# A hybrid attention and feed-forward step: the last two phases put in one block, with the feed-forward's first tiles in attention memory that is no longer read

## The chip, the cores and the metric

One core of one Trainium2 chip. The metric is the device time of one execution, in microseconds (us), taken as the median of several executions. The profile is one further execution under the hardware profiler.

## What is computed

One layer of a streaming encoder, for a prompt of 2048 rows and for 32 rows of a running stream, all of width 1024 and all in fp32. A matmul operand is split into a high and a low part, and every product is three matmuls (high·high, high·low, low·high).

```
h = rmsnorm(x, norm_mix_pre);  z = h @ w_in         # cut into the two groups' q, k, v, gate
ret_out  = silu(rg) * rms(retention(rq, rk, rv))    # 4 heads, width 512
diff_out = differential_attention(dq, dk, dv)       # 4 heads, width 512, block-causal mask
mix = concat(ret_out, diff_out) @ w_out
x   = x + rmsnorm(mix, norm_mix_post)               # "x1" below
u   = rmsnorm(x, norm_ffn_pre) @ w_up               # 1024 -> 4096
f   = square(relu(u)) @ w_down                      # 4096 -> 1024
y   = x + rmsnorm(f, norm_ffn_post)
```

## The kernel before

The kernel has four phases: retention, the projections of the attention group with the decode rows' attention, the prompt's attention with the output projection (`mix_phase`), and the feed-forward (`ffn_phase`). Each phase owns its SBUF tensors and semaphores and one block, in which each engine runs its own instruction stream. At the end of a phase (`phase`, L30) the semaphores are cleared and all engines meet at a barrier (L36).

**Attention (`mix_phase`).** Rows go in 16 tiles of 128 and each tile has four heads, so there are 64 items. One item is scores, exponentials, combination, transposes of the weights, and the weighted sum of V (`weigh`, L1493) which counts up `s_o`. The output projection of one tile of mixed rows j is a transpose (`mixT`, L1448), the split into `mTh` on ScalarE (L1221) and `mTl` on VectorE (`mT_lo`, L1354), and four quarters of 12 matmuls (`quarter`, L1465): quarters 0 and 1 fill the left 512 columns in bank `Y`, quarters 2 and 3 the right. j = 0 is the 32 decode rows, j = 16 is the last 128 prompt rows; below these last rows are "row tile 16". After each half ScalarE copies `Y` out (`y_out`, L1235), then sums squares (`meansq_y`, L1240); GpSimd takes the root (`rstd_y`, L1157); VectorE scales (`y_norm`, L1363) and adds the residual (`residual`, L1370), which gives x1. SyncE stores x1 to a scratch in HBM (`finish`, L1119) and waits for that store, and then loads the next residual rows (`residual_rows`, L1115) once ScalarE has read the buffer (`meansq_x`, L1248). GpSimd's `rstd_x` (L1163) leaves the root of each x1 row for the feed-forward. These tensors are live to the end: the w_out splits, the mixed rows, `mTh`, `mTl`, `xr`, `y`, the gain. Dead once the last `weigh` has run are `KT`, `V`, `S`, `AT`, `kn`, `qn`, `qT`, 114 KB per partition by their shapes.

**The tail of attention,** after the last item, is written by hand in program order on each engine. TensorE: quarters 2 and 3 of row tile 15, `mixT` of row tile 16, its four quarters. ScalarE: `y_out` and `meansq_y` of 15, `mTh` of 16, `meansq_x` of 15, then `y_out` (twice), `meansq_y`, `meansq_x` of 16. VectorE: `y_norm` and `residual` of 15, `mT_lo` of 16, `y_norm` and `residual` of 16.

**The feed-forward (`ffn_phase`).** The 17 row tiles are in two blocks, tiles 0 to 7 and tiles 8 to 16. For each block all the weights are read once, in 16 groups of 256 hidden columns. SyncE loads x1 tiles into four slots (`x_tile`, L1666), the gain (L1672) and half-pieces of weights into `raw`. Per row tile: VectorE normalises (`norm_x`, L1886), TensorE transposes (`x_transpose`, L2056, two banks of four), ScalarE writes `hTh` (`x_hi`, L1762), VectorE writes `hTl` (`x_lo`, L1892). The two transpose banks are single: `x_transpose(t)` waits for `x_lo(t-1)`. Weights are split by ScalarE (`up_hi`, L1751) and VectorE (`up_lo`, L1873). The first group's up products (`first_up`, L2065, four units of 24 matmuls for block 0) are woven with the transposes of tiles 4 to 7; behind each unit run `relu` (ScalarE, L1782), `square` (VectorE, L1913), `hid_hi` (ScalarE, L1787) and `hid_lo` (VectorE, L1919). After that TensorE alternates a group's up and down products (L2065, L2101), and VectorE adds the down products into `facc` (L1940).

The order at the start of block 0, which the change touches, is on VectorE:

```
norm_x(0) norm_x(1) x_lo(0) norm_x(2) x_lo(1) norm_x(3) up_lo(0) x_lo(2) norm_x(4) x_lo(3) norm_x(5)
x_lo(4) norm_x(6) square(0) x_lo(5) norm_x(7) hid_lo(0) x_lo(6) square(1) x_lo(7) hid_lo(1) ...
```

On ScalarE it is x_hi(0), x_hi(1), up_hi, x_hi(2) to x_hi(4), relu(0), x_hi(5), hid_hi(0), x_hi(6), relu(1), x_hi(7), hid_hi(1). On TensorE it is transposes 0 to 3, half of first_up(0), transpose 4, the other half, transpose 5, half of first_up(1), transpose 6, the other half, transpose 7, first_up(2), first_up(3).

Of the kernel before, what the change touches and what calls it, by code (L numbers as in the profile page):

```python
# [8 lines left out]
F32 = mybir.dt.float32  # L9
# [34 lines left out]
class Kept:  # L44


    def __init__(self, nc, tiles):
        self.ident = nc.alloc_sbuf_tensor("kept_ident", [P, P], F32)
        self.rstd_x = nc.alloc_sbuf_tensor("kept_rstd_x", [P, tiles], F32)
# [888 lines left out]
def mix_phase(nc, banks, keep, seq, dec, x_p, x_s, q_scratch, ret_scratch, mixd_scratch, k_p, v_p, w_out, gain,  # L938
# [8 lines left out]
    with phase(nc) as ctx:  # L947
        def sb(name, shape, dt=F32):
            return ctx.enter_context(nc.sbuf_tensor(f"mix_{name}", shape, dt))

        def sem(name):
            return nc.alloc_semaphore(f"mix_{name}")

        SP_, T, O, Y = banks[0:4], banks[4:6], banks[6], banks[7]
        wt = Weights(nc, ctx, "mixw", 2, 8, staged=False)
        KT = sb("KT", [P, 4, seq])
        V = sb("V", [P, nt, N])
        Sall = sb("S", [P, 4 * seq])
        S = [[Sall[:, (2 * b + m) * seq:(2 * b + m + 1) * seq] for m in range(2)] for b in range(2)]

        assert nt >= 10
        wt.raw = [V[:, nt - 8 + 4 * i:nt - 4 + 4 * i, :] for i in range(2)]
        AT = sb("AT", [P, nt, P])
        kn = [sb(f"kn{u}", [P, N]) for u in range(2)]
        qn = sb("qn", [P, N])
        qTs = [sb(f"qT{u}", [P, 4, P]) for u in range(2)]
        mix = sb("mix", [P, 1024])
        mTh, mTl = sb("mTh", [P, 8, P], F32R), sb("mTl", [P, 8, P], F32R)
        xr, y, gain_b = sb("xr", [P, 1024]), sb("y", [P, 1024]), sb("gain", [P, 1024])
        oscs, junk = [sb(f"osc{b}", [P, HD]) for b in range(2)], sb("junk", [P, 1024], BF16)  # L970
        half = sb("half", [P, 1])
        mx = [sb(f"mx{b}", [P, 2, 5]) for b in range(2)]
        nm = [sb(f"nm{b}", [P, 2]) for b in range(2)]
        l = [sb(f"l{b}", [P, 2]) for b in range(2)]
        rl = [sb(f"rl{b}", [P, 2]) for b in range(2)]
        r = [sb(f"r{b}", [P, 1]) for b in range(2)]
        stats = sb("head_stats", [P, 4])
        sos, mos = [stats[:, b:b + 1] for b in range(2)], [stats[:, 2 + b:3 + b] for b in range(2)]
        ro = [sb(f"rstd_o{b}", [P, 1]) for b in range(2)]
        sy, my, ry = sb("sy", [P, 1]), sb("my", [P, 1]), sb("ry", [P, 1])  # L980
        sx, mean_x = sb("sx", [P, 1]), sb("mean_x", [P, 1])

        s_gain, s_half, s_pad = sem("gain_loaded"), sem("half_set"), sem("padding_set")
        s_kq = [sem("kq_loaded0"), sem("kq_loaded1")]
        s_q = sem("q_loaded")
        s_vl = [sem(f"v_loaded{t}") for t in range(nt)]
        s_ret = sem("ret_loaded")
        s_x = sem("x_loaded")
        s_x1 = sem("x1_ready")
        s_stored = sem("x1_stored")  # L990
        s_ktr = sem("k_and_q_transposed")
        s_tfree = [sem("T0_free"), sem("T1_free")]
        s_qk = sem("pair_bank_filled")
        s_sc = sem("pair_bank_read")
        s_neg = sem("masked_corner_set")
        s_nm = sem("neg_max")
        s_e = sem("exp")
        s_rl, s_r = sem("recip_sums"), sem("ratio")
        s_A = sem("combined")
        s_ATp = sem("AT_psum")  # L1000
        s_o = sem("o_psum")
        s_osc = sem("o_scaled")
        s_so, s_mo, s_ro = sem("o_sumsq"), sem("o_meansq"), sem("o_rstd")
        s_mix = sem("mix_head")
        s_mTh = sem("mixT_hi")
        s_yp, s_y = sem("y_psum"), sem("y_sbuf")
        s_sy, s_my, s_ry, s_yn = sem("y_sumsq"), sem("y_meansq"), sem("y_rstd"), sem("y_normed")
        s_sx, s_mx, s_rx = sem("x1_sumsq"), sem("x1_meansq"), sem("x1_rstd")

        wv = w_out.rearrange("(k p) n -> k p n", p=P)  # L1010
        kv = k_p.rearrange("(n p) h d -> n p (h d)", p=P)
        vv = v_p.rearrange("(n p) h d -> n p (h d)", p=P)
        qv = q_scratch.rearrange("(n p) c -> n p c", p=P)
        rv = ret_scratch.rearrange("(n p) c -> n p c", p=P)
        xv = x_p[0].rearrange("(n p) d -> n p d", p=P)
        x1v = x1_scratch.rearrange("(n p) d -> n p d", p=P)

        def rows(j):
            return P if j else dec

        def width(t):
            return (t + 1) * P

        def chunks(t):
            return [(c, min(N, width(t) - c)) for c in range(0, width(t), N)]

        def groups(t):
            return [range(g, min(g + 4, t + 1)) for g in range(0, t + 1, 4)]

        def early(n):  # L1030
# [1201 lines left out]
```

## Time and profile before

| | us |
|---|---|
| median of 3 executions (lowest, highest) | 3084.81 (3082.12, 3088.74) |
| the profiled execution: its own time | 3086.13 |
| its span, first to last instruction | 3084.4 |
| mean granted TensorE clock | 0.972 |

| engine | busy us | share of the span | instructions |
|---|---|---|---|
| TensorE, matmul | 2897.8 | 94% | 14977 |
| TensorE, weight load | 2386.1 | 77% | 14977 |
| VectorE | 1493.9 | 48% | 3000 |
| ScalarE | 925.3 | 30% | 1838 |
| GpSimd | 286.0 | 9% | 420 |

All times are from the start of the span. In a timeline row the columns are start, duration, engine (PE is TensorE, PEld its weight load, DVE is VectorE, ACT is ScalarE, POOL is GpSimd, SPq is SyncE's DMA queue), the line of the kernel, the instruction, "output <- inputs", the shape, the count of merged instructions, and in brackets the engine's idle time before it with what ended it. A granted clock of 1.00 is 2.4 GHz and 0.50 is 1.2 GHz.

### The profile page before, as it was taken

The page shows a single profiled execution, that of the slowest core. Times are in us where ns is not written, and L with a number is a line of the kernel's source. Part 1 is how long each engine was busy: PE and PEld are TensorE (multiplying, and loading weights), DVE is VectorE, ACT ScalarE, POOL GpSimd, SP SyncE. Part 2 cuts the span into 40 slices and gives each one's busy share as a digit, 9 for nine tenths or more (in the row PEclk, how much of TensorE's full clock was granted, in tenths as well). Part 3 has the DMA queues.
Part 4 walks back from the last instruction along what each step waited for, and adds up shares of the span by engine and source line. Part 5 has one row for each costly group of instructions (what it writes and reads, how often), then busy time and mean ns, then how long its engine had stood idle before and what let it go on. Part 6 is the DMA issues. An engine that isn't in the chain of part 4 may idle for free.

```text
span 3084.4 us, 39331 instructions
## 1 busy us (share of the span) xinstructions
PE 2897.8 (94%) x14977; PEld 2386.1 (77%) x14977; DVE 1493.9 (48%) x3000; ACT 925.3 (30%) x1838; POOL 286.0 (9%) x420
## 2 busy tenths in 40 slices
PE   5999996899978999999699999999989999999997
PEld 4888885677856777766578888888879899898895
DVE  3223332333236877777444454444465444544446
ACT  3222222222125666666322111211132111121112
POOL 0122211111112111110000000000021000000003
PEclk8999998899989999999799999999999999999998
DMA  4111102332432211110321111111133111111112
GB/s 148 35 34 34 34 21 85 129 120 96 145 104 99 80 59 55 56 37 27 115 83 43 54 45 50 41 54 41 41 118 103 55 41 41 41 46 49 41 55 99
DMA packets 105660, 204.63 MB, mean 66 GB/s; under 512 B 11024, under 2 KB 47888, under 8 KB 105552
## 3 DMA queue, kind: packets, MB, share of 16 engines
q1 hardware_dynamic: 103248, 194.79, 19.1%
q0 software_dynamic: 2304, 8.39, 0.8%
q8 instruction: 69, 1.13, 0.1%
q14 instruction: 39, 0.32, 0.0%
HBM read 168.28 MB, written 34.87 MB: 66 GB/s over the span
## 4 chain that ended last, share of the span: by engine, by line
PE 48%; DVE 2%; DMA 0%; ACT 0%; issue 0%; SPq 0%
PE bank L2101 24%; PE bank L2065 23%; DVE ffn_facc L1899 1%; PE bank L2056 0%; DVE ffn_upl L1873 0%; DVE ffn_facc L1940 0%; DVE ffn_hTl L1892 0%; DVE ffn_x L1886 0%; DMA ffn_raw<-in_w_up_dram 0%; DMA ffn_gain_x<-in_norm_ffn_pre_dram 0%; DVE ffn_dnl L1880 0%; DMA ffn_x<-x_scratch 0%; ACT ffn_hTh L1762 0%; ACT ffn_relu L1782 0%; DVE ffn_facc L1906 0%
## 5 line engine op out<-in xcount | busy, mean ns | idle before, releaser
L1940 DVE TENSOR_TENSOR ffn_facc<-bank,ffn_facc 128x512 f32<-128x512 f32 x510 | 346.1, 689 | 243.7 <-PE bank L2101 242.5
L2065 PE MATMUL bank<-ffn_hTh,ffn_uph 128*128 128x352 f32 (+1 forms) x1280 | 451.0, 352 | 8.7 <-DVE ffn_upl L1873 5.5
L2065 PE MATMUL bank<-ffn_hTl,ffn_uph 128*128 128x352 f32 (+1 forms) x1280 | 449.6, 351 | 0.0
L2065 PE MATMUL bank<-ffn_hTh,ffn_upl 128*128 128x352 f32 (+1 forms) x1280 | 449.3, 351 | 0.0
L2101 PE MATMUL bank<-ffn_dnh,ffn_hidh 128*128 128x512 f32 x1088 | 430.3, 396 | 9.4 <-DVE ffn_dnl L1880 6.2
L2101 PE MATMUL bank<-ffn_dnh,ffn_hidl 128*128 128x512 f32 x1088 | 430.9, 396 | 0.0
L2101 PE MATMUL bank<-ffn_dnl,ffn_hidh 128*128 128x512 f32 x1088 | 429.9, 395 | 0.0
L1913 DVE SCALAR_TENSOR_TENSOR ffn_relu<-bank,ffn_relu 128x352 f32<-128x352 f32 (+1 forms) x160 | 94.6, 591 | 484.4 <-ACT ffn_relu L1782 484.2
L2065 PEld LDWEIGHTS bank<-ffn_hTh,ffn_uph 128*128 128x128 f32 x1280 | 241.1, 188 | 33.7 <-issue 7.7
L2065 PEld LDWEIGHTS bank<-ffn_hTl,ffn_uph 128*128 128x128 f32 x1280 | 241.3, 188 | 23.7
L2065 PEld LDWEIGHTS bank<-ffn_hTh,ffn_upl 128*128 128x128 f32 x1280 | 241.0, 188 | 22.6
L2101 PEld LDWEIGHTS bank<-ffn_dnh,ffn_hidh 128*128 128x128 f32 x1088 | 205.8, 189 | 59.3 <-DVE ffn_dnl L1880 6.9
L1757 ACT ACTIVATE ffn_dnh<-ffn_raw 128x1024 fp32r<-128x1024 f32 x64 | 64.5, 1053 | 616.7 <-PE bank L2101 605.5
L1782 ACT ACTIVATE ffn_relu<-bank 128x352 f32<-128x352 f32 (+1 forms) x160 | 82.8, 517 | 535.7 <-PE bank L2065 535.7
L2101 PEld LDWEIGHTS bank<-ffn_dnl,ffn_hidh 128*128 128x128 f32 x1088 | 205.2, 189 | 47.8
L2101 PEld LDWEIGHTS bank<-ffn_dnh,ffn_hidl 128*128 128x128 f32 x1088 | 205.3, 189 | 47.5
L185 PE MATMUL bank<-retw_whi,retp_hTh 128*128 128x512 f32 x544 | 216.8, 399 | 25.7 <-DVE ret_rope_b L395 16.6
L185 PE MATMUL bank<-retw_whi,retp_hTl 128*128 128x512 f32 x544 | 213.8, 393 | 0.0
L185 PE MATMUL bank<-retw_wlo,retp_hTh 128*128 128x512 f32 x544 | 213.7, 393 | 0.0
L1303 DVE TENSOR_SCALAR_CACHE_REDUCE mix_S<-bank 128x512 f32<-128x512 f32 (+4 forms) x320 | 175.0, 582 | 64.6 <-PE bank L1437 31.5
L185 PE MATMUL bank<-dpw_whi,dpp_hTh 128*128 128x512 f32 x408 | 164.4, 403 | 8.9 <-DVE dpw_wlo L175 8.9
L1203 ACT ACTIVATE mix_S<-mix_S,mix_nm 128x128 f32<-128x128 f32 (+15 forms) x128 | 153.7, 1201 | 45.2 <-DVE mix_nm L1317 44.9
(196 smaller groups left out, 4392.3 us busy)
## 6 DMA issues: line engine op xcount, KB each, us to landing
ffn_raw<-in_w_up_dram SPq DMA_DIRECT2D x64, 512.0 KB, 4.4
ffn_raw<-in_w_down_dram SPq DMA_DIRECT2D x64, 512.0 KB, 4.1
ffn_x<-x_scratch SPq DMA_DIRECT2D x24, 512.0 KB, 4.3
retp_x<-in_x_prompt_dram SPq DMA_DIRECT2D x16, 512.0 KB, 3.6
retw_raw<-in_w_in_dram SPq DMA_DIRECT2D x8, 1024.0 KB, 5.1
dpp_x<-in_x_prompt_dram SPq DMA_DIRECT2D x16, 512.0 KB, 4.9
dp_kst<-in_cache_diff_k_dram SPq DMA_DIRECT2D x32, 256.0 KB, 2.9
mix_xr<-in_x_prompt_dram SPq DMA_DIRECT2D x16, 512.0 KB, 3.3
```

The source lines that it names most:

```text
L185: last = self.nc.tensor.matmul(out, l[:, k, :], r[:, c, k, :], start=(k == 0 and q == 0), stop=(k == kt - 1 and q == 2))
L1203: nc.scalar.activation(S[n % 2][m][:, 0:width(t)], S[n % 2][m][:, 0:width(t)], ACT.Exp, bias=nm[n % 2][:, m:m + 1], accum_out=l[n % 2][:, ...
L1303: last = nc.vector.tensor_scalar(dst[:, c:c + whole], src[:, 0:whole], 1.0, None, ALU.mult, ALU.max, accum_out=mx[b][:, m, i + 1:i + 2])
L1757: nc.scalar.activation(dnh[:, i, :], raw[i][:], ACT.Copy).then_inc(s_whi, 1)
L1782: nc.scalar.activation(rh[i % 2][:, 0:w], bank[:, 0:w], ACT.Relu).then_inc(s_r, 1)
L1899: nc.vector.scalar_tensor_tensor(out=facc[:, i, :], in0=facc[:, i, :], scalar=rf[:, t:t + 1], in1=gain_b[:], op0=ALU.mult, op1=ALU.mult).t ...
L1913: nc.vector.scalar_tensor_tensor(out=rh[i % 2][:, 0:w], in0=bank[:, 0:w], scalar=0.0, in1=rh[i % 2][:, 0:w], op0=ALU.max, op1=ALU.mult).th ...
L1940: nc.vector.tensor_tensor(out=part, in0=Dn[i % s.rd][:], in1=part, op=ALU.add).then_inc(s_add, 1)
L2065: last = nc.tensor.matmul(bank[:, 0:w], l[:, k, f * P:(f + 1) * P], r[:, k, c:c + w], start=(k == 0 and q == 0), stop=(k == 7 and q == 2))
L2101: last = nc.tensor.matmul(Dn[i % s.rd][:], l[:, c:c + P], r[:, f, n * N:(n + 1) * N], start=(f == 0 and q == 0), stop=(f == FG - 1 and q = ...
```

## The change

`mix_phase` and `ffn_phase` become two stages of one block. Each engine's stream for attention is a generator that stops at named points of its tail; the feed-forward's stream resumes it at chosen places, so the two orders are woven together per engine. The barrier and the semaphore clearing between the two phases are gone. Everything before the tail keeps its order.

The memory of the feed-forward starts at the address of attention's. `hTh`, `hTl`, the x slots, `gain_x`, `raw`, `uph`, `upl` and the second gain come first (114 KB by their shapes) and lie in the dead tensors; `hid`, `relu`, `dnh`, `dnl` lie in the w_out splits; `facc` lies over the rest. Small tensors are packed, `half` is shared, and `rstd_x` has one column more.

The woven orders, attention's steps in brackets:

- SyncE: wait for the last `weigh`; x tile 0, gain, x tiles 1 to 3, first up pieces; [store x1 of 15, load residual rows of 16]; x tiles 4 to 7; [store x1 of 16]; second gain; second up pieces; x tiles 8 to 11.
- VectorE: norm_x(0); [mT_lo of 16]; norm_x(1); [y_norm and residual of 15]; x_lo(0), and on as before to hid_lo(0); [y_norm and residual of 16]; four memsets that stood at the phase's start; x_lo(6), and on as before.
- ScalarE: [y_out, meansq_y of 15, mTh of 16]; x_hi(0), x_hi(1), up_hi; [meansq_x of 15, y_out left half of 16]; x_hi(2), x_hi(3); [y_out right half, meansq_y of 16]; x_hi(4), relu(0), x_hi(5), hid_hi(0); [meansq_x of 16]; x_hi(6), and on as before.
- TensorE: [quarters of 15, mixT of 16]; transposes 0 and 1; [quarters 0 and 1 of 16]; transposes 2 and 3; [quarters 2 and 3 of 16]; first_up(0), and on as before.
- GpSimd: attention's stream, then the feed-forward's.

```diff
-    with phase(nc) as ctx:                      # in mix_phase and in ffn_phase
+    U, Dn = (banks[0:4] if before_it.last_pair == 0 else banks[2:4] + banks[0:2]), banks[4:8]
 def sync(sp, mixing):
+        sp.wait_ge(s_o, ntot)                   # the last weigh
+        yield "attention ended"
         finish(nt - 1)
         residual_rows(nt)
+        yield "last rows asked for"
         finish(nt)
...
+        next(mixing)
         x_tile(0)
         sp.dma_start(gain_x[:], gain_pre.to_broadcast([P, 1024])).then_inc(s_gain, 16)
         for t in (1, 2, 3):
             x_tile(t)
         for i in range(2):
             piece_up(0, i)
+        next(mixing)
         for t in (4, 5, 6, 7):
             x_tile(t)
+        next(mixing, None)
+        sp.wait_ge(before_it.s_rx, before_it.roots)
+        sp.dma_start(gain_b[:], gain_post.to_broadcast([P, 1024])).then_inc(s_gain_f, 16)
 def vector(dve, mixing):
+        next(mixing)                            # to the last mix_head
+        dve.wait_ge(s_gain, 16)
         norm_x(0)
+        next(mixing)                            # mT_lo(nt)
         norm_x(1)
+        next(mixing)                            # y_norm(nt - 1), residual(nt - 1)
         x_lo(0)
...
         hid_lo(s, 0, 0, 0, fu)
+        next(mixing, None)                      # y_norm(nt), residual(nt)
+        for e in range(2):
+            for part in range(2):
+                nc.vector.memset(hidden_flat[e][part][:, FG * tokens:].bitcast(F32), 0.0).then_inc(s_pad, 1)
         x_lo(6)
...
         down_lo(w0 + 4)
+        if s.b == 0:
+            dve.wait_ge(before_it.s_stored, before_it.stores)
+            dve.wait_ge(before_it.s_rx, before_it.roots)
 def scalar(act, mixing):
+        next(mixing)                            # to mT_hi(nt)
         x_hi(0)
         x_hi(1)
         up_hi(1)
+        next(mixing)                            # meansq_x(nt - 1), y_out(nt, 0)
         x_hi(2)
         x_hi(3)
+        next(mixing)                            # y_out(nt, 1), meansq_y(nt)
         x_hi(4)
         relu(s, 0, 0, fu)
         x_hi(5)
         hid_hi(s, 0, 0, 0, fu)
+        next(mixing, None)                      # meansq_x(nt)
         x_hi(6)
 def tensor(pe, mixing):
+        next(mixing)                            # to mixT(nt)
+        pe.wait_ge(before_it.s_sc, before_it.read_pairs)
+        x_transpose(0)
+        x_transpose(1)
+        next(mixing)                            # quarters 0, 1 of nt
+        x_transpose(2)
+        x_transpose(3)
+        next(mixing, None)                      # quarters 2, 3 of nt
         first_up(s, 0, range(0, 4))
...
+        pe.wait_ge(before_it.s_y, before_it.halves)
+def mix_ffn_phase(nc, banks, keep, mix_args, ffn_args):
+    with phase(nc) as ctx:
+        keep.s_half = nc.alloc_semaphore("half_set")
+        with ExitStack() as first:
+            mix = mix_stage(nc, first, banks, keep, *mix_args)
+        ffn = ffn_stage(nc, ctx, banks, keep, mix, *ffn_args)
+        with nc.Block() as block:
+            @block.sync
+            def _(sp):
+                ffn.sync(sp, mix.sync(sp))
...
```

## Rows read from the trace of the kernel before

**Rows 1.** The page: shares of the chain that ended last, by engine.
```profile
PE 48%; DVE 2%; DMA 0%; ACT 0%; issue 0%; SPq 0%
```

**Rows 2.** Busy time by stretch: stretch, length, each engine's busy us and count, clock, DMA.
```profile
1497.00:1505.00 8.00, 7.64 (x24) 5.87 (x24) 0.11 (x1) 0.39 (x3) 0.55 (x1) 0.73 0.32 118
1505.00:1511.00 6.00, 5.45 (x24) 4.43 (x24) 0.00 (x0) 0.50 (x1) 0.00 (x0) 1.00 0.00 0
1511.00:1527.00 16.00, 0.29 (x2) 0.00 (x0) 3.84 (x7) 3.30 (x7) 1.20 (x3) 0.62 0.41 143
1527.00:1541.00 14.00, 7.79 (x32) 6.18 (x32) 12.88 (x16) 6.45 (x10) 0.00 (x0) 0.50 0.80 294
1600.00:2200.00 600.00, 600.00 (x2589) 485.49 (x2588) 279.77 (x383) 113.97 (x161) 0.00 (x0) 1.00 0.15 47
```

**Rows 3.** TensorE's waits, 1484 to 1577: total us, times, longest.
```profile
PE bank L2056 <- DVE ffn_x L1886: 16.2, 1, 16.2
PE bank L1465 <- DVE mix_mTl L1354: 5.7, 1, 5.7
PE bank L2065 <- DVE ffn_upl L1873: 5.5, 1, 5.5
PE bank L2056 <- DVE ffn_hTl L1892: 4.3, 3, 2.9
```

**Rows 4.** Timeline of the tail of attention.
```profile
1481.71 2.84 PE L1493 MATMUL bank<-mix_V,mix_AT 128*128 128x128 f32 x24
1484.33 0.33 SPq L1115 DMA_DIRECT2D mix_xr<-in_x_prompt_dram  x1
1492.54 1.06 ACT L1221 ACTIVATE mix_mTh<-bank 128x512 fp32r<-128x512 f32 x2
1493.30 1.28 DVE L1363 SCALAR_TENSOR_TENSOR mix_y<-mix_y,mix_ry,mix_gain 128x1024 f32<-128x1024 f32 x1 [6.66 <-POOL mix_ry L1157]
1494.68 1.23 DVE L1370 TENSOR_TENSOR mix_xr<-mix_xr,mix_y 128x1024 f32<-128x1024 f32 x1
1495.83 1.28 DVE L1354 TENSOR_TENSOR mix_mTl<-bank,mix_mTh 128x512 fp32r<-128x512 f32 x2
1516.64 1.06 ACT L1248 ACTIVATE mix_junk<-mix_xr 128x1024 bf16<-128x1024 f32 x1 [3.31 <-DVE mix_xr L1370]
1518.10 0.55 POOL L1163 TENSOR_TENSOR kept_rstd_x<-mix_mean_x,mix_half 128x1 f32<-128x1 f32 x1 [4.14 <-ACT mix_mean_x L1252]
```

**Rows 5.** Timeline of the start of the feed-forward.
```profile
1520.85 0.43 SPq L1672 DMA_DIRECT2D ffn_gain_x<-in_norm_ffn_pre_dram  x1
1526.13 2.54 DVE L1886 SCALAR_TENSOR_TENSOR ffn_x<-ffn_x,kept_rstd_x,ffn_gain_x 128x1024 f32<-128x1024 f32 x2 [5.01 <-DMA ffn_gain_x<-in_norm_ffn_pre_dram]
1527.47 1.97 PE L2056 MATMUL bank<-kept_ident,ffn_x 128*128 128x128 f32 x8 [16.18 <-DVE ffn_x L1886]
1541.04 0.76 PE L2065 MATMUL bank<-ffn_hTh,ffn_uph 128*128 128x512 f32 x1 [1.50 <-DVE ffn_hTl L1892]
1546.02 1.04 PE L2056 MATMUL bank<-kept_ident,ffn_x 128*128 128x128 f32 x8
1546.66 1.09 ACT L1762 ACTIVATE ffn_hTh<-bank 128x512 fp32r<-128x512 f32 x2 [6.48 <-PE bank L2056]
1553.52 0.68 DVE L1919 TENSOR_TENSOR ffn_hidl<-ffn_relu,ffn_hidh 128x512 fp32r<-128x512 f32 x1
1559.78 0.50 PE L2065 MATMUL bank<-ffn_hTh,ffn_uph 128*128 128x512 f32 x1 [1.74 <-DVE ffn_hTl L1892]
```

**Rows 6.** The two issues of `raw` between 1519 and 1535, us to landing.
```profile
DMA to landing us min/median/max: 8.8/9.2/9.7
```

**Rows 7.** Timeline of a restart of TensorE near the end of the kernel.
```profile
3037.01 0.58 PE L2101 MATMUL bank<-ffn_dnh,ffn_hidh 128*128 128x512 f32 x1 [3.54 <-DVE ffn_dnl L1880]
3037.39 0.63 PE L2101 MATMUL bank<-ffn_dnl,ffn_hidh 128*128 128x512 f32 x1
3037.82 0.63 PE L2101 MATMUL bank<-ffn_dnh,ffn_hidl 128*128 128x512 f32 x1
```

More of the change, by code:

```diff
@@ new lines, in mix_stage @@
+    AT = sb("AT", [P, nt, P])
+    kn = [sb(f"kn{u}", [P, N]) for u in range(2)]
+    qn = sb("qn", [P, N])
+    qTs = [sb(f"qT{u}", [P, 4, P]) for u in range(2)]
+    assert nt >= 10
+    wt = Weights(nc, ctx, "mixw", 2, 8, staged=False)
+    wt.raw = [V[:, nt - 8 + 4 * i:nt - 4 + 4 * i, :] for i in range(2)]
+    mix = sb("mix", [P, 1024])
+    mTh, mTl = sb("mTh", [P, 8, P], F32R), sb("mTl", [P, 8, P], F32R)
+    xr, y, gain_b = sb("xr", [P, 1024]), sb("y", [P, 1024]), sb("gain", [P, 1024])
@@ new lines, in mix_stage, with pair_banks, plan_transposes, bank_of @@
+    plan_pairs()
+    def pair_banks(u):
+        return SP_[2 * (u % 2)], SP_[2 * (u % 2) + 1]
+    t_use = {}
+    def plan_transposes():
+        i = itertools.count()
+        t_use["k", 0], t_use["q", 0] = next(i), next(i)
+        for n, (t, h) in enumerate(items):
+            for g in range(len(groups(t))):
+                t_use["A", n, g] = next(i)
+            if h == 0 and t + 1 < nt:
+                t_use["k", t + 1], t_use["q", t + 1] = next(i), next(i)
+    plan_transposes()
+    def bank_of(use):
+        return T[t_use[use] % 2]
@@ new lines, in ffn_stage @@
+    uph, upl = sb("uph", [P, 8, GW], F32R), sb("upl", [P, 8, GW], F32R)
+    gain_b = sb("gain_f", [P, 1024])
+    hidden_flat = [[sb(f"hid{n}{u}", [P, FG * tokens + P - dec], F32R) for n in "hl"] for u in range(2)]
+    rh = [sb(f"relu{i}", [P, N]) for i in range(2)]
+    dnh, dnl = sb("dnh", [P, FG, 1024], F32R), sb("dnl", [P, FG, 1024], F32R)
+    facc = sb("facc", [P, nb_max, 1024])
+    junk = sb("junk", [P, 1024], BF16)
+    half = keep.half
+    stats = sb("stats", [P, 3, nt + 1])
+    sf, mf, rf = (stats[:, a, :] for a in range(3))
@@ new lines, in ffn_stage, with rows, columns, loads @@
+    dnv = [w_down.rearrange("(g f p) n -> f g p n", p=P, f=FG)[i] for i in range(FG)]
+    def rows(t):
+        return P if t < nt else dec
+    def columns(t):
+        c = (t - (b1[0] if t in b1 else 0)) * P
+        return slice(c, c + rows(t))
+    slots = {t: t % 4 for t in range(12)}
+    slots.update({t: t % 2 for t in range(12, nt + 1)})
+    def loads(t):
+        return sum(slots[a] == slots[t] for a in range(t + 1))
+    def before(t):
+        return max((a for a in range(t) if slots[a] == slots[t]), default=None)
@@ new lines, in ffn_stage, with steps @@
+    shapes = [Shape(0), Shape(1)]
+    for b, s in enumerate(shapes):
+        s.u0 = sum(a.ku * G for a in shapes[:b])
+        s.d0 = sum(a.kd * G for a in shapes[:b])
+        s.t0 = s.tiles[0]
+    def steps(eng, step):
+        step(0, 0, False, False)
+        step(1, 1, False, False)
+        with eng.Fori(1, G // 2 - 1) as j:
+            for e in range(2):
+                step(2 * j + e, e, False, False)
+        step(G - 2, 0, False, True)
+        step(G - 1, 1, True, True)
+    by_dve = nb_max - 3
@@ new lines, in residual, with store @@
+    def residual(eng, queue, b, i):
+        t = blocks[b][i]
+        if b == 0 and i < 2:
+            eng.wait_ge(s_xT, 2 * (10 + i) + 2)
+        elif b and i - 2 >= by_dve:
+            eng.wait_ge(s_yd, i - 1 - by_dve)
+        else:
+            eng.wait_ge(s_y, t - 1 if i >= 2 else b1[0])
+        queue.dma_start(xe[i % 2][0:rows(t), :], x1v[t][0:rows(t), :]).then_inc(s_xe[b][i % 2], 16)
+    def store(eng, queue, b, i):
+        t = blocks[b][i]
+        if b and i >= by_dve:
+            eng.wait_ge(s_yd, i + 1 - by_dve)
+        else:
+            eng.wait_ge(s_y, t + 1)
+        if i >= 2:
+            eng.wait_ge(s_st[b][i % 2], 16 * (i // 2))
+        queue.dma_start(yv[t] if t < nt else y_s[0], facc[0:rows(t), i, :]).then_inc(s_st[b][i % 2], 16)
```

2061 lines of the change are left out of this document (1000 added, 1061 removed).

## The prediction

> **What bounds the kernel now.** I read the chain that ended last first: TensorE has nearly all of it that the page accounts for [rows 1]. The page's slices then show where TensorE is not full, and the table of stretches shows why the boundary matters: in the feed-forward's steady part TensorE is busy 600.00 of 600 us at clock 1.00 [rows 2], so nothing there can be gained or hidden. Around the boundary it is busy 0.29 of 16 us, then 7.79 of 14 us at half clock [rows 2]. TensorE's waits between 1484 and 1577 name the causes: 16.2 us for the first normalised x tile, 5.7 us for `mTl` of row tile 16, 4.3 us in three waits for `x_lo`, 5.5 us for the second up piece [rows 3]. The change can win the first three in part, and the fourth not at all: `uph` and `upl` are single, so their second piece can only be split after the last first_up in both kernels. Its cold restart stays too.
>
> I measure the result at one place, the start of first_up(2), at 1559.78 before [rows 5]. From there on the order is the same in both kernels, TensorE decides, and the loops are full. What is gained there is gained at the end.
>
> **Loads.** The last `weigh` ends at 1481.71 + 2.84 = 1484.55 and SyncE's queue is free at 1484.33 + 0.33 = 1484.66 [rows 4]. So the seven loads start at 1484.7 instead of 1520.5 (one load ahead of the gain's 1520.85 [rows 5]), and the gain is issued near 1485.1. Before, it ended VectorE's wait 5.3 us after its issue (1520.85 to 1526.13) [rows 5]. That gives 1490.4. The residual rows of 15 are issued just ahead, half a megabyte, which at 294 GB/s [rows 2] is 1.8 us, so 1492.2 at worst. norm_x(0) takes 2.54 / 2 = 1.27 [rows 5] and ends between 1491.7 and 1493.5. The up pieces, the last of the seven, land at most 9.7 us after their issue [rows 6] near 1487.5, at 1497.2. They are wanted at 1501. The store of x1 of 15 is issued near 1498.3, when that queue is empty again, so nothing holds it up.
>
> **mTl.** ScalarE writes `mTh` of 16 from 1492.54 to 1493.60 [rows 4], unchanged. Before, `mT_lo` stood behind y_norm (1.28) and residual (1.23) and ended at 1497.11 [rows 4]. Now it follows norm_x(0) and ends about 0.7 after the second half of `mTh`, at 1494.4. That is 2.7 us earlier.
>
> **Transposes 0 and 1.** Transpose 0 runs 1494.5 to 1496.5 at the low clock (1.97) [rows 5]. Transpose 1 waits for x_lo(0), and on VectorE that is now behind norm_x(1), y_norm and residual of 15: 1494.4 + 1.27 + 1.28 + 1.23 = 1498.2, then two halves of 0.7, so 1499.6. The second half of transpose 1 takes 1.0 more: 1500.6. So a wait of about 2.5 us takes the place of part of the old one.
>
> **Quarters 0 and 1.** 24 matmuls took 7.64 us from a cold start and 5.45 us warm [rows 2]. TensorE has had some work since 1494.5, with gaps. I take 7.1, nearer the cold row, as the gaps are about as long as the work: 1507.7. The bounds are 1506.1 and 1508.3. Meanwhile x_hi(1), up_hi, norm_x(2), x_lo(1), norm_x(3), up_lo and meansq_x of 15 fill ScalarE to about 1505 and VectorE to about 1506; all have ended before they are needed.
>
> **Transposes 2 and 3.** ScalarE takes y_out first (half of an x_hi by its size, so 0.6, to 1508.4), then x_hi(2) (1.09) [rows 5], and x_lo(2) follows to 1510.4. Transpose 3's second half ends at 1510.9. **Quarters 2 and 3**, warm, take 5.5: 1516.4. If the clock has dropped it is 7.6.
>
> **x tiles 4 to 7.** They are queued on SyncE behind a wait for meansq_x of 15, which is behind up_hi on ScalarE, so they are issued from 1505.4 on. With 5.3 us (the gain's row) tile 4 is there at 1510.7, VectorE's norm_x(4) ends at 1512.0 and x_lo(3) at 1513.4, 3 us before first_up(0) asks for it. A landing later than 8.3 us would delay TensorE one for one; the longest of [rows 6], with two pieces queued behind five loads, is 9.7, which would cost 1.4.
>
> **first_up(0).** It starts at 1516.4, not at 1541.04. Its first 12 matmuls ran cold before; warm they take half of 5.45 and a little, 2.8, so transpose 4 runs at 1519.3, not at 1546.02 [rows 5] (4.98 after 1541.04). The shift is 26.7 us.
>
> **The step given back.** After hid_lo(0), which ended at 1553.52 + 0.68 = 1554.20 in the old clock time [rows 5], VectorE now runs y_norm and residual of 16 (1.28 + 1.23 and a gap, to 1556.8) and four memsets of 96 columns, which lie under ScalarE's next step. ScalarE's meansq_x of 16 must wait for that residual, and x_hi(6) is queued behind it. From the start of meansq_x to GpSimd's root was 1518.10 - 1516.64 = 1.46 [rows 4]: ScalarE is free at 1558.2, x_hi(6) ends at 1559.3, x_lo(6) at 1560.2, transpose 7 at 1560.8, x_hi(7) and x_lo(7) at 1562.3. first_up(2) starts at 1562.4 instead of 1559.78: 2.6 us are given back. The unit before it ended near 1557, so TensorE has one transpose in 5.4 us. A wait of 1.74 us left the clock up (the matmul after it takes 0.50) [rows 5], one of 3.54 us did not (0.63 and starts 0.43 apart) [rows 7]. I take the low clock: 8 matmuls at 0.2 more each is 1.7 us. The bound on the other side is nothing.
>
> **What else moves.** SyncE stores x1 of 16 only after that residual, and the second gain and the second up pieces queue behind the store: issued near 1559.5 and landed by 1569 with the 9.7 of [rows 6]; up_hi wants them after first_up(3), near 1576. That is hidden with 7 us to spare. The two new waits on VectorE after down_lo and the one on TensorE for `Y` are met by some 10 us. The barrier itself (from 1518.10 + 0.55 = 1518.65 [rows 4] to the first load near 1520.5) is inside the shift and not counted again. Addresses of all feed-forward tensors change; the trace cannot price that, between nothing and the rival below.
>
> **Sum.** 26.7 - 2.6 - 1.7 = 22.4 us. The profiled execution took 3086.13, so 3063.7; the median of the three shown is 1.3 lower, so **3062.4**.
>
> **A rule against the row.** Waits on work of VectorE around 3 us long are what this boundary has left, and one of 3.54 us dropped the clock [rows 7]. The Trainium skill, TensorE: Matmul & The Clock Gate, section Loop structure matters more than you think, says the reverse of such waits: VectorE's copy out of PSUM "doesn't break PE warmth", and it is the long wait for a DMA that does. By that rule the clock is never lost at transpose 7, and the sum is 24.1; the row, where the wait was for VectorE, speaks against it.
>
> **Rivals.**
>
> 1. *The clock stays up* where I take it as low. Quarters 0 and 1 in 5.45 (1.6 gained), the transposes before them 1.5 shorter in all, and no cold start at first_up(2) (1.7). That gives 27.2 us and 3057.6. For it is the 1.74 us wait, against it [rows 7]. Chance 0.15, with the page's rule in it.
> 2. *The clock stays down* through the whole weave, as the work between 1494 and 1516 is broken four times. Quarters 2 and 3 then cost 2.2 more, quarters 0 and 1 0.5, the two late transposes 1 and the 24 matmuls of first_up(0) up to 4.8: 8.5 us less, 13.9 us, 3070.9. For it is the stretch 1527 to 1541, where TensorE was busy 7.79 of 14 us and stayed at 0.50 [rows 2]. Against it: 5.45 us without a gap come first. Chance 0.22.
> 3. *Slower than before.* The feed-forward's operands lie at other addresses. TensorE is full there, with 2589 matmuls in 600 us [rows 2], 232 ns each; by the code 16 x (96 + 96) + 16 x (144 + 108) = 7104 run after the boundary. If each took over 3.2 ns more (1.4%), the whole 22.4 us would be gone, and at 7 ns the kernel is at 3112. Against it: quarters 0 and 1 in attention's layout have 24 in 5.45 us, 227 ns, nearly the same pace [rows 2]. Chance 0.03.
> 4. *It doesn't do what it says.* If SyncE's seven loads are not early, because the residual rows' wait holds the queue, the first x tile comes no sooner than before and only mTl's 2.7 us and the barrier's 1.8 us are won: 3080. The order in SyncE's stream speaks against it. Chance 0.04.
>
> The forecast itself, 18 to 26 us won, has 0.56.
>
> **How the numbers follow.** The range must take in rivals 1 and 2 with the spread of the three executions (3082.12 to 3088.74), 3 us to each side: 3054 to 3074. About 0.2% (6 us) is what a measurement of this kernel can tell from no change. Faster by more than that: forecast and rivals 1 and 2, 0.93; within it: rival 4, 0.04; slower: rival 3, 0.03.
>
> **What would show it.** The gain's load ends VectorE's wait near 1491, transpose 0 starts near 1494.5, and quarters 0 and 1 start near 1500.6 behind x_lo(0). first_up(0) starts near 1516 at full clock. Behind hid_lo(0) ScalarE waits about 2.6 us for the residual of 16 and TensorE about 3 us for x_lo(6). first_up(2) starts near 1536 (1559.78 less 24) and the next matmuls show 0.43 us between starts. The pace from there to the end is 232 ns per matmul as before. It would be wrong if transposes 0 and 1 started well after 1495, if x tile 4 came late, or if the steady loops changed their pace.

## The result, and the profile after

The changed kernel takes 3063.11 us in the median (3062.47 to 3065.07, 4 executions), the kernel before 3083.47 in the same comparison. The ratio is 0.9932 with a 95% interval of 0.9915 to 0.9950: 20.4 us won, 0.7%. Forecast were 3062.4 us, with a range of 3054 to 3074. The profiled execution took 3065.07 us, its span is 3063.3, where the old one had 3084.4.

TensorE's waits from 1484 to 1556 of the changed kernel answer to [rows 3]. The columns are the total in us, the number of waits and the longest.

```profile
PE bank L2082 <- DVE ffn_hTl L1912: 6.0, 3, 2.4
PE bank L2091 <- DVE ffn_upl L1893: 5.6, 1, 5.6
PE bank L2082 <- DVE mix_mTl L1360: 3.0, 1, 3.0
PE bank L2091 <- DVE ffn_hTl L1912: 1.5, 1, 1.5
```

The 16.2 us for the first x tile are gone, and the 5.7 us for `mTl` are 3.0. The 5.5 us for the second up pieces are there as 5.6. The waits for `x_lo` in front of transposes have grown from 4.3 to 6.0 us: this is what took the place of the old ones. The timeline shows where they sit, and answers to [rows 4] and [rows 5].

```profile
1484.93 0.37 SPq L1685 DMA_DIRECT2D ffn_x<-x_scratch  x1
1485.34 0.43 SPq L1689 DMA_DIRECT2D ffn_gain_x<-in_norm_ffn_pre_dram  x1
...
1490.77 1.03 PE L1456 MATMUL bank<-kept_ident,mix_mix 128*128 128x128 f32 x8
1491.60 1.28 DVE L1906 SCALAR_TENSOR_TENSOR ffn_x<-ffn_x,kept_rstd_x,ffn_gain_x 128x1024 f32<-128x1024 f32 x1 [4.63 <-DMA ffn_gain_x<-in_norm_ffn_pre_dram]
1493.50 1.29 DVE L1360 TENSOR_TENSOR mix_mTl<-bank,mix_mTh 128x512 fp32r<-128x512 f32 x2 [0.61 <-ACT mix_mTh L1225]
1494.85 1.97 PE L2082 MATMUL bank<-kept_ident,ffn_x 128*128 128x128 f32 x8 [3.04 <-DVE mix_mTl L1360]
1498.42 1.28 DVE L1912 TENSOR_TENSOR ffn_hTl<-bank,ffn_hTh 128x512 fp32r<-128x512 f32 x2
1499.25 1.94 PE L2082 MATMUL bank<-kept_ident,ffn_x 128*128 128x128 f32 x8 [2.44 <-DVE ffn_hTl L1912]
...
1530.34 1.06 ACT L1252 ACTIVATE mix_junk<-mix_xr 128x1024 bf16<-128x1024 f32 x1 [4.78 <-DVE mix_xr L1376]
1532.24 1.29 DVE L1912 TENSOR_TENSOR ffn_hTl<-bank,ffn_hTh 128x512 fp32r<-128x512 f32 x2 [1.51 <-ACT ffn_hTh L1779]
1533.08 1.16 PE L2082 MATMUL bank<-kept_ident,ffn_x 128*128 128x128 f32 x8 [2.33 <-DVE ffn_hTl L1912]
1535.72 0.79 PE L2091 MATMUL bank<-ffn_hTh,ffn_uph 128*128 128x512 f32 x1 [1.48 <-DVE ffn_hTl L1912]
1536.31 0.63 PE L2091 MATMUL bank<-ffn_hTl,ffn_uph 128*128 128x512 f32 x1
```

The loads now go out 35.5 us earlier. The gain's load ends VectorE's wait at 1491.60, and `mT_lo` waits for ScalarE and no longer for y_norm and residual. Then transpose 1 waits 2.44 us for x_lo(0). Near 1530, ScalarE's `meansq_x` of the last rows waits for their residual, x_hi(6) stands behind it, and TensorE waits 2.33 and 1.48 us. The matmul behind that takes 0.79 and its successor 0.63: the low clock (granted 0.50 from 1535.7 to 1538.7).

**A measure that leaves out the first half of the kernel.** `mixT` of row tile 16 started between 1485.17 and 1490.77 in the fourteen profiles, though nothing ahead of it on TensorE differs in order. So I compare distances from that start. "First" is to the start of first_up(2), "units" from there to the next group of 96 up products, "group" the time of those 96, and "all" from `mixT` to the end of the span. All are differences of start times in the timelines and chains. Medians are of the timed executions, "less" is against the kernel before in the same session (for "before" itself the row is the profile and median shown ahead of the prediction). One slow execution of the kernel before, 6028 us long, is left out in the session of r_after, r_busy, r_best and e9_fill, where the kernel before is then at 3083.70 us.

| kernel | first | units | group | all | median | less |
|---|---|---|---|---|---|---|
| before | 69.36 | 16.86 | 23.98 | 1593.98 | 3084.81 | |
| changed | 44.95 | 18.36 | 24.85 | 1572.53 | 3063.11 | 20.4 |
| changed, again (r_after) | 44.68 | 19.82 | 24.08 | 1572.88 | 3062.92 | 20.8 |
| e1_join | 65.33 | 17.04 | 24.05 | 1590.31 | 3081.49 | 3.0 |
| e2_loads | 55.96 | 17.03 | 25.12 | 1583.03 | 3071.64 | 12.8 |
| e3_late | 42.45 | 17.01 | 24.95 | 1569.04 | 3059.73 | 24.7 |
| e4_quarters | 41.10 | 18.64 | 24.97 | 1569.51 | 3059.89 | 24.6 |
| e5_both | 38.13 | 17.00 | 24.21 | 1563.44 | 3055.36 | 31.6 |
| e6_busy | 45.02 | 17.03 | 23.93 | 1570.19 | 3063.66 | 23.3 |
| r_busy | 45.21 | 18.53 | 24.91 | 1573.53 | 3062.16 | 21.5 |
| e7_mtlo | 45.66 | 19.71 | 24.02 | 1573.83 | 3062.36 | 24.6 |
| e8_best | 37.09 | 17.12 | 24.02 | 1562.06 | 3055.96 | 31.0 |
| r_best | 37.09 | 17.03 | 24.61 | 1563.39 | 3053.70 | 30.0 |
| e9_fill | 37.20 | 17.04 | 22.52 | 1561.14 | 3050.26 | 33.4 |

The 95% intervals of the ratios are 3 us to each side for e1_join (0.9982 to 1.0001) and 4 to 6 us for the others, so a median alone can't settle a difference of 1 us. The column "first" repeats within 0.3 us for the same kernel and can.

### The profile page after: what moved, and what is told of

It reads as the page before. It is cut to its first block, busy times and chain, and to the rows that moved or that the text cites. A ratio compares the mean times of both kernels' runs of the same rounds, so it can differ in the third digit from the quotient of the medians.

```text
span 3063.3 us, 39308 instructions
## 1 busy us (share of the span) xinstructions
PE 2900.1 (95%) x14977; PEld 2388.8 (78%) x14977; DVE 1493.1 (49%) x3000; ACT 925.0 (30%) x1838; POOL 286.7 (9%) x419
## 4 chain that ended last, share of the span: by engine, by line
PE 64%; DVE 4%; ACT 1%; issue 1%; DMA 1%; POOL 0%; SPq 0%; DVEq 0%; ACTq 0%
PE bank L2127 24%; PE bank L2091 23%; PE bank L1473 6%; PE bank L1445 4%; PE bank L1501 3%; PE bank L1486 2%; DVE ffn_facc L1919 1%; PE bank L1420 0%; DVE mix_S L1336 0%; DVE mix_S L1309 0%; POOL mix_head_stats L1157 0%; PE bank L1456 0%; PE bank L2082 0%; DVE ffn_facc L1960 0%; DVE ffn_hTl L1912 0%
```

## The experiments

**What the parts are worth: e1_join and e2_loads.** In both, an engine that is not woven runs its attention stream to the end first.

```diff
+def drained(gen):
+    for _ in gen:
+        pass
+    return itertools.repeat(None)
-                ffn.tensor(pe, mix.tensor(pe))
+                ffn.tensor(pe, drained(mix.tensor(pe)))      # both runs; the same on ScalarE and VectorE
-                ffn.sync(sp, mix.sync(sp))
+                ffn.sync(sp, drained(mix.sync(sp)))          # e1_join only
```

> Both stages in one block at the new addresses, but nothing is woven: on every engine all of attention's stream comes first, and SyncE's loads for the feed-forward come after the last store. Theory (the parts add as in the prediction): only the barrier and the earlier mT_lo are won. mTl of row tile 16 is ready near 1494.3 instead of 1497.1, so everything behind it is 2.8 us earlier; the first feed-forward load follows the store's landing, near 1516.5 instead of 1520.5. Gain over the kernel before: about 4 us, some 3079.5. Rival 1 (the joining itself, the barrier with its semaphore clearing, is most of the gain): over 10 us gained, under 3073. Rival 2 (the new addresses cost something in the full loops): the loops' up and down groups of 96 matmuls take more than 22.28 and 22.25 us, and the kernel is at 3084 or more.

Measured: 3081.49 us, ratio 0.9991 (0.9982 to 1.0001), so the median alone does not set it apart from the kernel before; "first" is 4.0 us shorter. Quarter 0, and the timeline behind the last residual:

```profile
1491.36 0.79 PE L1473 MATMUL bank<-mixw_whi,mix_mTh 128*128 128x512 f32 x1 [3.04 <-DVE mix_mTl L1360]
...
1510.38 0.33 SPq L1122 DMA_DIRECT2D x_scratch<-mix_xr  x1
1513.03 0.33 SPq L1685 DMA_DIRECT2D ffn_x<-x_scratch  x1
1518.65 2.52 DVE L1906 SCALAR_TENSOR_TENSOR ffn_x<-ffn_x,kept_rstd_x,ffn_gain_x 128x1024 f32<-128x1024 f32 x2 [8.30 <-DMA ffn_gain_x<-in_norm_ffn_pre_dram]
1520.09 1.94 PE L2082 MATMUL bank<-kept_ident,ffn_x 128*128 128x128 f32 x8 [15.05 <-DVE ffn_x L1906]
```

TensorE still waits 15.05 us for the first x tile. Joining by itself, with the earlier `mT_lo`, is worth what the theory said, and the rival that the barrier is the cost falls. Of the 4.0 us, 2.7 are the wait for `mTl` (3.04 instead of 5.70 [rows 3]), which comes of the order on VectorE and not of the joining; 1.1 are the shorter wait for the first x tile (15.05 instead of 16.18). The full loops take 22.28 and 22.25 us for 96 matmuls in every kernel with the new addresses, as before (22.25 to 22.28 us in the chains of all of them), so the rival about addresses falls too.

> As the changed kernel on SyncE (seven loads right after the last weigh, x tiles 4 to 7 ahead of the last store), but ScalarE, VectorE and TensorE run all of attention first and the feed-forward after it. Theory: the wait for the first loads is gone and nothing else. Quarters of row tile 16 end near 1508.2, its residual on VectorE near 1513.5, norm_x(0) follows at once and ends near 1514.8, transpose 0 starts there, cold, instead of at 1527.5: 12.6 us earlier, then the old order with its cold first_up(0). Gain over the kernel before about 12.6 us, some 3071; so early loads are worth 8 to 9 us over joining alone and weaving another 8 us. Rival (the woven tail only hides work that was hidden anyway, the loads are all of it): 20 us gained, some 3063 as the changed kernel.

Measured: 3071.64 us, ratio 0.9955 (0.9938 to 0.9971); "first" is 13.4 us shorter, 0.8 more than worked out. TensorE's wait for the first x tile is now the residual's and the normalisation's, not the load's:

```profile
PE bank L2082 <- DVE ffn_x L1906: 6.7, 1, 6.7
```

So the early loads are worth 65.33 - 55.96 = 9.4 us beyond joining, and the woven order 55.96 - 44.95 = 11.0 us at "first", of which the slower units give 1.3 us back in this profile of the changed kernel and 2.8 in r_after.

**The step given back: e3_late.**

```diff
         hid_lo(s, 0, 0, 0, fu)
-        next(mixing, None)                  # y_norm(nt), residual(nt)
...
         hid_lo(s, 0, 0, 1, fu)
+        next(mixing, None)
         hid_hi(s, 0, 0, 0, fu)              # on ScalarE
-        next(mixing, None)                  # meansq_x(nt)
...
         hid_hi(s, 0, 0, 1, fu)
+        next(mixing, None)
         for t in (4, 5, 6, 7):              # on SyncE
             x_tile(t)
+        for i in range(2):
+            sp.wait_ge(s_wlo, 1 + i)
+            piece_up(1, i)
         next(mixing, None)
...
-            for i in range(2):              # the same two pieces, where they stood
+            for i in range(2 if s.b else 0):
```

> The changed kernel with the last rows' y_norm and residual (VectorE) moved from behind hid_lo(0) to behind hid_lo(1), meansq_x of row tile 16 (ScalarE) from behind hid_hi(0) to behind hid_hi(1), and the second up pieces' loads ahead of the last x1 store on SyncE. Theory (the step given back): first_up(2) starts 2.3 to 2.6 us earlier after a wait of about 1.7 us and at the full clock, which is worth 1.35 us more on its 48 matmuls. So 3.6 to 4.0 us less than the changed kernel, about 3059.3. Rival 1 (the clock falls there whatever the gap): 2.5 us less, 3060.6. Rival 2 (the late store or the second gain's load delays something behind them): no gain or a loss, 3063 or more, with a wait of ScalarE for the second up pieces.

Measured: 3059.73 us; "first" 2.5 us shorter, the units 17.01 instead of 18.36. The restart there:

```profile
1530.91 0.50 PE L2094 MATMUL bank<-ffn_hTh,ffn_uph 128*128 128x512 f32 x1 [1.74 <-DVE ffn_hTl L1915]
```

A wait of 1.74 us as in [rows 5], and 0.50 us, not 0.79. Both halves of the theory hold, and ScalarE's wait for a residual that stood behind y_norm on VectorE is what the give-back was.

**The waits between transposes: e4_quarters.**

```diff
-                x_transpose(0)
-                x_transpose(1)
-                next(mixing)                # quarters 0, 1
-                x_transpose(2)
-                x_transpose(3)
-                next(mixing, None)          # quarters 2, 3
+                for t in range(4):
+                    x_transpose(t)
+                    next(mixing)            # one quarter
```

> The changed kernel with the four transposes set between the four quarters of row tile 16 (transpose 0, quarter 0, transpose 1, quarter 1, and so on) instead of two transposes ahead of two quarters. The order on the other engines is unchanged. Theory: the waits of 2.4 and 1.2 us for x_lo(0) and x_lo(2) lie under a quarter. Quarter 0 starts near 1496.8 instead of 1500.85, the last quarter ends near 1513.6 instead of 1517.0: 3.4 us less, about 3059.7, with the give-back behind hid_lo(0) unchanged. Rival (the waits only move: quarter 2 waits for y_out, transpose 3 for x_lo(2), and the clock stays low for longer): under 1.5 us less, 3061.6 or more.

Measured: 3059.89 us, "first" 3.85 us shorter. Transposes 1, 2 and 3 don't wait; quarter 2 now waits 0.76 us for `y_out`, as the rival said, but the others are gone. VectorE shows a new wait:

```profile
1506.69 1.29 DVE L1904 SCALAR_TENSOR_TENSOR ffn_x<-ffn_x,kept_rstd_x,ffn_gain_x 128x1024 f32<-128x1024 f32 x1 [2.38 <-DMA ffn_x<-x_scratch]
1509.32 0.47 PE L2089 MATMUL bank<-ffn_hTh,ffn_uph 128*128 128x512 f32 x1 [0.16 <-DVE ffn_hTl L1910]
```

x tile 4 was just late enough to hold first_up(0) by 0.16 us. The prediction had given it 3 us to spare in the changed kernel; this order uses them up.

**Both: e5_both.** The edits of e3_late and e4_quarters.

> The moves of e3_late and e4_quarters together, on the changed kernel. Theory (two separate waits, so they add): from mixT of row tile 16 to first_up(2), e3_late took 2.5 us off the changed kernel's 44.95 and e4_quarters 3.85; both give 38.6 us and the full clock at first_up(2). By the medians 3.4 and 3.2 us, so about 3056.5. Rival (x tile 4 is the bound now: in e4_quarters VectorE already waited 2.4 us for its load): first_up(0) can't come earlier and only one of the gains shows, 3059 or more.

Measured: 3055.36 us, ratio 0.9903 (0.9886 to 0.9919); "first" is 38.13, where the sum of the two gave 38.6. They add.

**The price of the late mT_lo: e7_mtlo.**

```diff
         yield "mixed rows complete"
-        mT_lo(nt)
-        yield "mixed rows split"
         y_norm(nt - 1)
         residual(nt - 1)
+        mT_lo(nt)
+        yield "mixed rows split"
```

> The changed kernel with mT_lo of row tile 16 back behind y_norm and residual of row tile 15 on VectorE, as before the change; norm_x(0) stays ahead of them and norm_x(1) comes after. Theory (the wait for x_lo(0) has taken the place of most of the old one): mTl is ready 2.6 to 2.9 us later, transpose 0 starts that much later, but x_lo(0) was behind the same two steps anyway, so quarter 0 starts only 1.0 to 1.3 us later. Loss against the changed kernel 1.0 to 1.3 us, about 3064.3. Rival (the early mT_lo was worth its whole 2.7 us): 3065.8.

Measured in the profile: transpose 0 waits twice as long, and transpose 1 hardly at all:

```profile
1488.67 1.03 PE L1456 MATMUL bank<-kept_ident,mix_mix 128*128 128x128 f32 x8
1495.74 1.97 PE L2082 MATMUL bank<-kept_ident,ffn_x 128*128 128x128 f32 x8 [6.04 <-DVE mix_mTl L1360]
1498.36 1.94 PE L2082 MATMUL bank<-kept_ident,ffn_x 128*128 128x128 f32 x8 [0.65 <-DVE ffn_hTl L1912]
```

From `mixT`, transpose 0 starts 3.0 us later than in the changed kernel (7.07 against 4.08), transpose 1 only 1.2 us later (9.69 against 8.48) and quarter 0 as well, as the theory had it. First_up(2) is 0.7 to 1.0 us later (45.66 against 44.95 and 44.68). So the early `mT_lo` is worth about 1 us of its 2.7 there, as the wait for x_lo(0) would have come anyway. The medians don't show it: 3062.36 is below the changed kernel's 3063.11 in another session, within the intervals.

**The clock at first_up(2): e6_busy and its repeat.**

```diff
                 first_up(s, 1, range(4, 8))
+                for _ in range(8):
+                    nc.tensor.matmul(Dn[0][:], uph[:, 0, 0:P], hTh[:, 0, 0:N], start=True, stop=True)
                 x_transpose(7)
```

> The changed kernel with 8 more matmuls of 512 columns (results not used, into a bank that is free) on TensorE just ahead of transpose 7, in its wait of 2.3 us for x_lo(6). Theory (the low clock at first_up(2) comes from TensorE's lack of work in that wait): the matmuls take 1.9 us of the wait, first_up(2) starts where it did, and its 48 matmuls take 11.4 us instead of 12.8; about 1.4 us less than the changed kernel, 3061.7. Rival (the wait for x_lo(7), or where the matmuls fall in time, sets it): 12.8 us as before and no gain, 3063.

> e6_busy once more. Theory (filled wait, so no low clock): the 48 matmuls take 11.4 us again, and the median is 1.4 us or more below r_after. Rival: 12.8 us or more in this execution, and no difference between the medians.

The first profile agreed with the theory, the repeat did not. First e6_busy, then r_busy, the same program:

```profile
1529.08 2.01 PE L2150 MATMUL bank<-ffn_hTh,ffn_uph 128*128 128x512 f32 x8
1531.59 1.16 PE L2082 MATMUL bank<-kept_ident,ffn_x 128*128 128x128 f32 x8 [0.50 <-DVE ffn_hTl L1912]
1534.23 0.50 PE L2091 MATMUL bank<-ffn_hTh,ffn_uph 128*128 128x512 f32 x1 [1.48 <-DVE ffn_hTl L1912]
```

```profile
1525.23 2.02 PE L2150 MATMUL bank<-ffn_hTh,ffn_uph 128*128 128x512 f32 x8
1527.74 1.16 PE L2082 MATMUL bank<-kept_ident,ffn_x 128*128 128x128 f32 x8 [0.49 <-DVE ffn_hTl L1912]
1530.38 0.79 PE L2091 MATMUL bank<-ffn_hTh,ffn_uph 128*128 128x512 f32 x1 [1.48 <-DVE ffn_hTl L1912]
```

The waits are the same to 0.01 us, yet in one the 48 matmuls take 11.43 us and in the other 12.93. The medians, 3063.66 and, beside r_after's 3062.92, 3062.16, show no gain. The theory that the filled wait keeps the clock up is not borne out. The second wait, 1.48 us for x_lo(7), was not filled, so the rival that names it stands. Without filling the clock was low in all four profiles with this order (changed, r_after, e4_quarters, e7_mtlo), with it in one of two, which is too few to tell.

**The changed kernel again: r_after.** No edit.

> The changed kernel once more, unchanged, for its profile and its time beside the others of this group. Theory (the length of TensorE's low clock after the same wait differs from one execution to the next): from mixT of row tile 16 to first_up(2) 44.5 to 45.5 us as before, but the 48 matmuls of first_up(2) and (3) and the next 96 take other times than 12.76 and 24.85 us, each within the 11.4 to 14.1 and 23.9 to 25.2 us that the profiles so far show. Rival (the order of the program fixes it): 12.76 and 24.85 again, within 0.1 us.

Measured: "first" 44.68, but 14.21 us for the 48 matmuls instead of 12.76, and 24.08 instead of 24.85 for the 96. The restart is the same as in the first profile, and only lasts longer:

```profile
1532.90 0.80 PE L2091 MATMUL bank<-ffn_hTh,ffn_uph 128*128 128x512 f32 x1 [1.48 <-DVE ffn_hTl L1912]
1533.50 0.63 PE L2091 MATMUL bank<-ffn_hTl,ffn_uph 128*128 128x512 f32 x1
```

14.21 lies 0.1 outside the span of values that I had named; what matters is that neither repeats.

**A faster version: e8_best, r_best.** The edits of e5_both and these:

```diff
         x_hi(0)                             # on ScalarE
-        x_hi(1)
-        up_hi(1)
         next(mixing)                        # meansq_x(nt - 1) alone; y_out(nt, 0) at the next stop
+        up_hi(1)
+        x_hi(1)
+        next(mixing)
         norm_x(2)                           # on VectorE
+        up_lo(0)
         x_lo(1)
         norm_x(3)
-        up_lo(0)
```

> e5_both, and on ScalarE meansq_x of row tile 15 straight behind x_hi(0), where ScalarE waited 2.9 us, with up_hi ahead of x_hi(1); on VectorE up_lo ahead of x_lo(1). So the residual rows of 16 and x tiles 4 to 7 are asked for some 4 us earlier and y_out is not held up. Theory: quarter 2's wait of 0.8 us for y_out goes and x tile 4 no longer bounds; 0.7 to 1.5 us less than e5_both, about 3055.5. Rival (the store and residual rows ahead of x tiles were not late enough to matter): as e5_both within 0.3 us.

> e8_best once more, for its time beside the changed kernel. Theory: 7 to 8 us below r_after, about 3056. Rival (part of that was the chip or the session): under 5 us below.

"First" is 37.09 in both profiles, 1.04 less than e5_both, and quarter 2's wait for `y_out` and VectorE's for x tile 4 are gone. The medians are 3055.96 beside e5_both's 3055.36 in one session, and 3053.70 beside the changed kernel's 3062.92 in the other: 9.2 us less, where 7 to 8 were expected. Against the kernel before the ratio is 0.9904 (0.9890 to 0.9918). The gain over e5_both is seen in the profile alone.

**The low clock as a cost: e9_fill.** e8_best with matmuls whose results are not used in the two longest waits.

```diff
+    me.w = wt.hi                            # in mix_stage
...
+                for _ in range(12):
+                    nc.tensor.matmul(Dn[0][:], before_it.w[:, 0, 0, 0:P], before_it.w[:, 0, 0, :], start=True, stop=True)
                 pe.wait_ge(before_it.s_sc, before_it.read_pairs)
...
                 first_up(s, 3)
+                for _ in range(22):
+                    nc.tensor.matmul(Dn[0][:], hTh[:, 0, 0:P], hTh[:, 0, 0:N], start=True, stop=True)
                 pe.wait_ge(s_pad, 4)
```

> e8_best with TensorE kept at work in its two longest waits by matmuls whose results are not used: 12 in the wait of 3.0 us for mTl of row tile 16, 22 in the wait of 5.6 us for the second up pieces. Theory (the low clock after these waits is a cost of its own): the 96 matmuls after the second wait take 22.3 us instead of 24.0, and transposes 0, 1 and quarters 0, 1 run at the full clock; 1.7 us less than r_best where the clock had stayed up at the first wait, up to 5 us where it had not; about 3053. Rival (the extra matmuls delay what follows, or the clock falls all the same): no gain, or the group behind the wait starts later by more than 0.3 us.

Measured: 3050.26 us (3048.45 to 3051.35), ratio 0.9890 (0.9874 to 0.9906), 3.4 us below r_best in the same session; all five executions lie below all five of r_best (3051.55 to 3055.17). The restarts:

```profile
1489.25 2.98 PE L2140 MATMUL bank<-mixw_whi 128*128 128x512 f32 x12
1492.62 1.09 PE L2086 MATMUL bank<-kept_ident,ffn_x 128*128 128x128 f32 x8 [0.39 <-DVE mix_mTl L1361]
...
1542.70 0.47 PE L2095 MATMUL bank<-ffn_hTh,ffn_uph 128*128 128x512 f32 x1 [0.59 <-DVE ffn_upl L1897]
```

The clock is up at both, and the 96 matmuls take 22.52 us; they took 23.9 to 25.1 in every other kernel. At the first wait nothing follows from this profile alone: e8_best's transpose 0 took 1.09 with no filling and r_best's 1.97, after the same 3.04 us. "First" is 37.20, as it is 37.09 both in e8_best, where the clock was up at transpose 0, and in r_best, where it was not: other engines decide the path to first_up(2) in this order, and the clock costs nothing there. What the profile shows is a gain of 1.5 to 2.1 us at the second wait (22.52 against 24.02 and 24.61); the rest of the 3.4 us is within the intervals. The two fillings were not run apart.

## Why the prediction was right

**The shift to first_up(2)** was forecast as 26.7 - 2.6 = 24.1 us. From `mixT` it is 69.36 - 44.95 = 24.41. Step by step, with 0.35 us taken off the changed kernel's times since its `mixT` is that much later:

- Loads: VectorE's wait ended at 1491.25, between the 1490.4 and 1492.2 forecast.
- Transpose 0 at 1494.50 (forecast 1494.5); transpose 1 started at 1498.9, when the first half of x_lo(0) was done (1498.2 + 0.7 by the forecast's terms).
- Quarters 0 and 1 took 7.31 us from their first matmul to transpose 2 (7.1). In the five other profiles with this order it was 6.83 to 7.57, so that the hit is this close is luck; the bounds of 5.5 and 7.7 hold.
- Quarters 2 and 3 took 5.50 at the full clock (5.5), and first_up(0) started at 1516.86 - 0.35 = 1516.5 (1516.4).
- x tile 4 was there in time: norm_x(4) followed x_lo(2) without a wait.
- The give-back: e3_late shows 2.50 us (2.6), by the mechanism described. ScalarE waited 2.56 us past hid_lo(0) (2.6), and TensorE 2.33 us for x_lo(6) (3).

**The clock** was the term of the sum that was mis-sized. I took 1.7 us at first_up(2) from 8 matmuls. The two profiles of the changed kernel have 12.76 - 11.41 = 1.35 and 2.80 us there. The restart after the second up pieces, which the prediction said "stays", took 24.85 and 24.08 us, against 23.98 before, and the stretch from there to the last down group took 0.4 and 0.6 us more than before. So the 24.41 us of the first profile shrink to 21.45 at the end (1.50 in the units, 0.87 in the group, 0.42 in the stretch, 0.17 behind it), and r_after's 24.68 to 21.10 (2.96, 0.10, 0.60, and 0.08 back), 1.0 and 1.3 us short of the 22.4 forecast. Only the loss at first_up(2) comes with the change's order there: it is 1.35 in one execution and 2.80 in the next. The later terms, which I had put at nothing, can't be charged to the change: the group varies from 23.9 to 25.1 us in the thirteen profiles without filling and the stretch behind it from 1436.0 to 1437.3 in all fourteen, though the order there is the same, and the one profile of the kernel before is near the low end of both. So the mechanism and the place were right, and the size was not one number.

**The rule of the Trainium skill,** TensorE: Matmul & The Clock Gate, section Loop structure matters more than you think, that VectorE's copy out of PSUM doesn't break the warmth: at transpose 7 the waits are for such a step, and the low clock followed in both profiles of the changed kernel, in e4_quarters, e7_mtlo and r_busy, but not in e6_busy. So a wait for VectorE can be followed by the low clock here, with 1.35 to 2.80 us of loss, and the prediction was right not to rely on the rule. But it had carried the rule too far: the words of the Trainium skill stand in a loop whose next matmuls follow immediately, and here TensorE stood still for 2.33 and 1.48 us; of such a loop these runs show nothing. Nor was [rows 7] a test of it, as that wait was for the split of a down weight (L1880), which copies nothing out of PSUM. And the traces go just as much against reading a fixed length of wait from [rows 7].

**The rivals.** That the clock stays down throughout did not happen: quarters 2 and 3 took 5.46 to 5.50 us in the six profiles that have them in a row. That the clock stays up did not happen either in the changed kernel. Slower loops at other addresses: none. The loads were early, at 1484.93, so the fourth rival falls too. The forecast was off by 0.7 us in the median, which is less than the interval and in part luck: the gain was forecast as 22.4 us and measured as 20.4, but the kernel before was itself 1.3 us faster in that comparison than in the three executions that the forecast started from. The range of 20 us was wider than the unknown terms turned out.

**What the gain is made of**, at first_up(2): joining with the earlier `mT_lo` 4.0 us (2.7 of them the latter), early loads 9.4, weaving 11.0. The prediction gave no such split, and some 16 us of TensorE's waits around the boundary were still left in the changed kernel; 7.9 us at first_up(2) and 9.2 in the median could be taken from them by order alone.

## What to carry to other kernels

At a boundary between two stages the barrier is cheap, and what is dear is the time until the first loads and the first steps of each engine have gone through: here joining was 4 us, most of it one step moved forward, and loading ahead and weaving the two orders were 20. When two streams are woven, follow each engine's queue for the step that waits for another engine (here a sum of squares behind a residual): the steps behind it inherit the wait, and moving it behind the next unit's steps won 2.5 us. Put the transposes that depend on one another between independent matmuls and not in pairs ahead of them.

To compare orders of some microseconds, measure distances from a common instruction behind the part that varies; the start of `mixT` differed by up to 5.6 us between these profiles through work that no edit touched.

## What the runs showed of the hardware that was not expected

The low clock after a wait is no fixed cost. The same program after the same waits (2.33 and 1.48 us) took 12.76 and 14.21 us for 48 matmuls; another one, 11.43 and 12.93. After the 3.04 us wait for `mTl`, transpose 0 took 1.97 us in six of nine profiles, 1.88 and 1.94 in two, and 1.09 in e8_best, whose repeat r_best has 1.97. After the 5.6 us wait it was low each time, but for 1.7 to 2.8 us of loss (23.9 to 25.1 us instead of 22.28). Behind a single wait of 1.73 or 1.74 us at first_up(2) the clock was up in all eight profiles that have one. Where two waits stood there instead, 2.3 us and then, behind one transpose, 1.4 to 1.5 us, it was low in all four profiles that had nothing filled in. What decides it is open: the traces show the waits and the result, not the cause.
